# Differential attention: one group of eight value products an iteration in place of two groups of four

## What is computed

```
sc = einsum('bqhmd,bkhmd->bmhqk', q, k) * scale + bias     # two maps m = 0, 1
p  = softmax(sc, axis=-1)
a  = p[:, 0] - lam * p[:, 1]
o  = einsum('bhqk,bkhd->bqhd', a, v)                       # v: 64 columns a head
```

## Time and profile before

| | |
|---|---|
| median of 3 runs | 4055.61 us (4053.83 to 4058.95) |
| span of the profiled execution | 4058.1 us; what lies around it isn't listed |
| differential attention, layer 1 | 1182.8 us (first scores) to 1695.6 us (last output) |
| differential attention, layer 2 | 3206.8 to 3720.2 us, by the same pattern |
| granted clock of TensorE in the stage (1215 to 1680 us) | 1.00 (the 2.4 GHz level) |
| busy in that stretch of 465 us | PE 419.88, DVE 422.11, ACT 378.65, POOL 451.55 us |

### The profile page before, as it was taken

How to read it: one execution, slowest core, us unless ns; L and a number is a source line. 1 busy time by engine, 2 the same in 40 slices (tenths; PEclk the granted TensorE clock), 3 DMA queues, 4 the chain that set the end, 5 groups by cost and what they waited for, 6 DMA issues and landing times. The chain is left out here.

```text
span 4058.1 us, 51537 instructions
## 1 busy us (share of the span) xinstructions
PE 3793.6 (93%) x19002; PEld 2623.3 (65%) x19002; DVE 2243.3 (55%) x3973; ACT 1659.8 (41%) x2886; POOL 2463.3 (61%) x1381
## 2 busy tenths in 40 slices
PE   8999999999989899889989999999999889998898
PEld 7789774555545666557777897755555456665577
DVE  3002125555569999875530030255555699998755
ACT  3112103333348888761031021033333588887610
POOL 1221326877769999855512213267777699997555
PEclk9999999999999999999999999999999999999999
DMA  5433535233320222235353334422333202223353
GB/s 177 127 130 121 145 129 124 60 92 74 78 59 1 57 57 58 66 104 187 135 177 122 133 114 142 140 68 55 72 72 72 59 1 57 57 58 71 105 179 135
DMA packets 180864, 392.43 MB, mean 97 GB/s; under 512 B 18014, under 2 KB 100168, under 8 KB 168968
## 3 DMA queue, kind: packets, MB, share of 16 engines
q1 hardware_dynamic: 179752, 387.75, 34.1%
q10 hardware_dynamic: 864, 1.41, 0.2%
HBM read 255.93 MB, written 135.67 MB: 96 GB/s over the span
## 5 line engine op out<-in xcount | busy, mean ns | idle before, releaser
L1297 POOL TENSOR_TENSOR mla_sum_pool<-mla_sum_pool,mla_probs 128x1024 f32<-128x1024 f32 (+1 forms) x336 | 777.6, 2314 | 209.4 <-ACT mla_probs L1258 184.4
L1315 DVE TENSOR_REDUCE carry_row_max<-psum 128x1 f32<-128x512 f32 x688 | 474.5, 690 | 415.7 <-PE psum L1130 410.7
L1258 ACT ACTIVATE mla_probs<-psum 128x1024 f32<-128x1024 f32 x384 | 373.3, 1021 | 693.8 <-PE psum L1167 686.6
L1613 ACT ACTIVATE diff_probs<-psum,diff_shift 128x1024 f32<-128x1024 f32 x512 | 566.5, 1112 | 186.2 <-DVE diff_shift L1697 180.5
L1690 DVE TENSOR_REDUCE diff_row_max<-psum 128x1 f32<-128x1024 f32 x512 | 611.6, 1218 | 44.5 <-PE psum L1534 37.5
L1560 PE MATMUL psum<-ident,diff_probs 128*128 128x128 f32 x2048 | 328.3, 284 | 104.3 <-DVE diff_turned L1724 66.9
L638 PE MATMUL psum<-in_x_hi,in_w_hi 128*128 128x512 f32 x1024 | 409.9, 400 | 2.7 <-ACT in_mla_val L745 2.7
L638 PE MATMUL psum<-in_x_hi,in_w_lo 128*128 128x512 f32 x1024 | 405.8, 396 | 0.0
L638 PE MATMUL psum<-carry_firsts,in_w_hi 128*128 128x512 f32 x1024 | 404.6, 395 | 0.0
L1560 PEld LDWEIGHTS psum<-ident,diff_probs 128*128 128x128 f32 x2048 | 215.9, 141 | 280.1 <-issue 178.2
L1180 PE MATMUL psum<-mla_probs,mla_v_op 128*64 128x512 f32 x1536 | 374.8, 609 | 0.0
(11 more groups left out here) (213 smaller groups left out, 7408.7 us busy)
## 6 DMA issues: line engine op xcount, KB each, us to landing
in_w_raw<-in_w_in SPq DMA_DIRECT2D x64, 512.0 KB, 3.9
split_d<-in_out SPq DMA_DIRECT2D x64, 512.0 KB, 2.7
raw_d<-in_out SPq DMA_DIRECT2D x32, 512.0 KB, 2.6
mq_d<-in_out SPq DMA_DIRECT2D x48, 256.0 KB, 3.6
mk_d<-in_out SPq DMA_DIRECT2D x48, 256.0 KB, 3.9
carry_firsts<-split_d SPq DMA_DIRECT2D x48, 256.0 KB, 8.0
carry_weights<-split_d SPq DMA_DIRECT2D x48, 256.0 KB, 7.7
carry_weights<-split_d SPq DMA_DIRECT2D x16, 768.0 KB, 18.0
```

Of the source, the lines that this page charges most:

```text
L1258: nc.scalar.activation(probs[:, s % RING, :].rearrange("p (a n) -> p a n", n=CH), psum[:, S0 + 2 * (s % 2):S0 + 2 * (s % 2) + 2, :], ACT.E ...
L1297: nc.gpsimd.tensor_tensor(acc, start, probs[:, s % RING, mine], ALU.add).then_inc(pool_added, 1)
L1315: nc.vector.tensor_reduce(row_max[:, u % 2, qb, n:n + 1], psum[:, sweep_bank(g), :], AX.X, ALU.max).then_inc(maxed, 1)
L1613: nc.scalar.activation(dst[:, half * HALF:(half + 1) * HALF].rearrange("p (a n) -> p a n", n=CH), banks(n, m, half), ACT.Exp, bias=shift[: ...
```

## The change

`products` loses its argument `place` and goes through both chunks of eight key blocks at once. It is called once an iteration, between scores(n,1,0) and turns(n-2,1).

```
-                def products(n, place):
-
-                    g = (n - 4) // 2
+                def products(n):
+
+                    g, half = divmod(n - 4, 2)
                     if not 0 <= g < GROUPS:
                         return
-                    b, chunk = g // (NB // 2) % 2, 2 * ((n - 4) % 2) + place
-                    if chunk == 0 and g >= 1:
+                    b = g // (NB // 2) % 2
+                    if half == 0 and g >= 1:
                         pe.wait_ge(o_ready, g)
-                    pe.wait_ge(*copies(2 * g + 1, chunk))
-                    for kb in range(4 * chunk, 4 * chunk + 4):
-                        e = kb % 2
-                        last = nc.tensor.matmul(psum[e * DV:(e + 1) * DV, PV, 0:2 * P], v_op[b][:, kb, :],
-                                                turned[:, g % 2, kb, :], start=(kb < 2), stop=(kb >= NB - 2))
-                    if chunk == 3:
+                    for chunk in (2 * half, 2 * half + 1):
+                        pe.wait_ge(*copies(2 * g + 1, chunk))
+                        for kb in range(4 * chunk, 4 * chunk + 4):
+                            e = kb % 2
+                            last = nc.tensor.matmul(psum[e * DV:(e + 1) * DV, PV, 0:2 * P], v_op[b][:, kb, :],
+                                                    turned[:, g % 2, kb, :], start=(kb < 2), stop=(kb >= NB - 2))
+                    if half == 1:
                         last.then_inc(pv_done, 1)
...
                     if on:
                         scores(n, 0, 1)
-                    products(n, 0)
                     turns(n - LAG, 0)
                     if on:
                         scores(n, 1, 0)
+                    products(n)
                     turns(n - LAG, 1)
                     if on:
                         scores(n, 1, 1)
-                    products(n, 1)
                     turns(n - LAG, 2)
```

## The result

The changed kernel takes 4212.98 us (median of 4 runs, 4208.04 to 4217.4) against 4056.74 us before: ratio 1.0389, 95% interval 1.0376 to 1.0402. It is slower, 156 us, by more than the 124 us of the forecast and 3 us beyond its range. The profiled execution has a span of 4206.2 us, 148.1 more than that of before.

The account below looks back on a forecast made before the run. GpSimd was taken to bound the differential stage at 7.84 us a unit; a ring lengthened to 8.87 us gave 60 x (8.87 - 7.84) = 62 us a layer, 124 for two, so 4180 us, range 4125 to 4210.

Parts of the forecast that it names:

- What bounds the kernel before: Differential stage: GpSimd is the bound, with 7.69 us of instructions a unit and 7.78 us from unit to unit.
- The ring: Closed waits through VectorE, ScalarE and TensorE, maximum of scores(n,1,1) to the next: 8.84 us heavy, 8.90 light, against 7.84.
- The places of the waits: Differential stage: new waits of TensorE for ScalarE's copy, VectorE for scores(n,1,1), GpSimd for ScalarE's scale; 0.4 to 1 us each.
- E + 8.1: E is the start of the maximum of scores(n,1,1); VectorE's maximum of scores(n,1,0) was to end 8.1 us later.
- The drain keeps its order ..., worth under 1 us a layer: End of the differential stage: order kept but for unit 62's first transposes, under 1 us a layer either way.
- granted clock 1.0: Listed among the signs that the forecast is right: the granted clock stays at 1.0.
- The bounds of the ring's terms: Uncertainty of products, copy latency and shift: 124 - 35 to 124 + 18 us over 120 intervals, so 4145 to 4198.
- The rule weighed: TensorE tiling mode: fewer switches save 0.25 us an iteration; by the rule alone the time would be 4026 us.
- the 60 intervals of the sum: Intervals of the ring in iterations 4 to 63 that hold products: 60 x (8.87 - 7.84) = 62 us a layer.
- 1: Rival: TensorE's own work sets the pace, so saved switches come off, 30 us, to 4026; chance 2%.
- 2: Rival: GpSimd hides all of the insertion, so the time stays at 4056; chance 6%.
- 3: Rival: ScalarE's copy is no link, the ring through VectorE's copy(n-3,2) is longest, 40 us more, 4096; chance 10%.

Follow-up runs that it names:

- h: Kernel before, with ScalarE scaling 640 columns of a unit and GpSimd 384, in place of 512 and 512: 4049.99 us.
- j: Kernel before, with TensorE doing scores(n,0,1) ahead of turns(n-3,3), division of the scaling unchanged: 4084.76 us.
- f: Changed kernel, with the two matmuls of scores(n,0,0) issued twice, ahead of the wait for VectorE's copy(n-3,2): 4185.33 us.
- a: Kernel before, groups of four kept, only the first moved from before turns(n-2,0) to before turns(n-2,1): 4081.19 us.
- g: Changed kernel, with four of the eight products of an iteration left out: 4081.48 us.
- c: Changed kernel, with the eight products in one piece behind scores(n,0,1), before turns(n-2,0): 4148.69 us.
- e: Changed kernel, with ScalarE's copy(n-2,3) between the two exps of map 1 in place of behind both: 4182.43 us.

## Why the prediction was wrong, point by point

- **What bounds the kernel before.** GpSimd's work, as the forecast has it, is right by 0.04 us alone: in h this work fell by 0.21 us a unit and the pace from 7.84 to 7.80, where something else holds it. That this is a ring through the other engines is likely by j's 8.09, but it wasn't followed step by step.
- **The ring** of 8.84 and 8.90 us: right, 8.85 in the iteration shown and 8.86 as the mean of f. Its slack of 0.96 us against 1.96 inserted is borne out by a, g and f. 2 x 59 x (8.86 - 7.84) = 120 us.
- **The places of the waits**: right, their sizes too small. GpSimd's new wait was put at about 1 us a unit and is 72.3 us in 51 (1.4, with the slow stretches in it; in f 60.7 in 52, 1.2). The wait of turns(n-2,0) for ScalarE's copy was put at 0.4 to 0.5 us and is 0.35 to 0.94, 35.9 us in 51. The wait of the maximum of scores(n,1,1) was put at 0.9 us an iteration, 50 us a layer, and is 74.2 us in 51 (1.45; in f 65.4 in 52, 1.26); the other 19 of the 93 us are the maximum of scores(n,0,1), which waited 17 us before. The forecast let the maximum of scores(n,1,0) end near E + 8.1, by the rows of a heavy iteration; in the light one shown it ends at E + 7.5 (1516.59 + 1.21).
- **"The drain keeps its order ..., worth under 1 us a layer"**: wrong. From unit 62's ratio to the end of the last output pass 18.0 us before and 22.2 and 23.7 after (f: 23.3 and 22.1). In layer 1, of the 4.2 us more, 1.4 come up to the last band matmuls (1678.34 before, 1753.71 after), in the last turn of the ring, which ends behind that ratio. From there to the last 16 products pass 15.55 us in place of 12.72. Behind the last scores the pieces of products stand at other places too. Before, two transposes wait, 1.15 + 0.79 us:

```profile
1681.49 0.63 PE L1560 MATMUL psum<-ident,diff_probs 128*128 128x128 f32 x4 [1.15 <-DVE diff_turned L1724]
...
1683.92 1.09 PE L1560 MATMUL psum<-ident,diff_probs 128*128 128x128 f32 x8 [0.79 <-DVE diff_probs L1731]
```

In the changed kernel four do, 1.86 + 1.28 + 0.34 + 0.34 us:

```profile
1756.68 0.63 PE L1560 MATMUL psum<-ident,diff_probs 128*128 128x128 f32 x4 [1.86 <-DVE diff_turned L1724]
1758.58 0.65 PE L1560 MATMUL psum<-ident,diff_probs 128*128 128x128 f32 x4 [1.28 <-ACT diff_turned L1631]
1759.16 3.56 PE L1576 MATMUL psum<-diff_turned,diff_v_op 128*64 128x256 f32 x16
1762.65 1.09 PE L1560 MATMUL psum<-ident,diff_probs 128*128 128x128 f32 x8
1764.09 1.16 PE L1560 MATMUL psum<-ident,diff_probs 128*128 128x128 f32 x8 [0.34 <-ACT diff_turned L1631]
...
1768.49 0.63 PE L1560 MATMUL psum<-ident,diff_probs 128*128 128x128 f32 x4 [0.34 <-ACT diff_turned L1631]
```

The waits are 1.9 us more. The 16 records take 3.56 us here and 1.95 in the ring above: from 1758 to 1763 us the granted clock is 0.66, behind the waits of 1.86 and 1.28 us. That is another 1.6 us. Against it, one piece of four less stands in this stretch (1.0 us); the 0.3 us that are left weren't followed.

- **"granted clock 1.0"**: wrong, and this is the step that failed. The bounds of the ring's terms allowed for 18 us more; the clock was put at nothing, without a reason. The runs showed 0.97 in the stage and a cost of 27 us (4213 against f's 4185, which lies in the range). The drains added another 10 us where under 2 were allowed; without either of the two the time would have been within the range. That waits alone lower the clock isn't shown: in c and e TensorE waits too (it is busy in 380 and 379 of 465 us, in the changed kernel in 370), and their clock stays at 1.00 between the ratios.
- **The account.** In the profiled executions the interval between ratios 3 and 62 grew by 72.6 and 71.5 us in the two layers, the drains by 4.2 and 5.7; that is 154, and the span grew by 148. The stretch between the two differential stages is 5.7 us shorter (1515.9 against 1521.6 us), and it is so in a and f too, and more so in h (1514.9), which leaves the products where they were; so it doesn't come from their place alone. Why stays open.
- **The rule weighed.** The Trainium skill, TensorEngine Tiling (Array Packing), Key Properties, has it that a change of tiling mode drains TensorE. The trace agrees that one pair of switches fewer saves time: one piece of eight takes 1.88 us, two of four 2 x 1.01. It was no guide to the result: the gain is a small part of 1 us in a ring that got 1.96 longer.
- **Slips in the working.** Products run to iteration 67, not 65; the 60 intervals of the sum don't hang on it. Of these, 59 were measured at the ring's length, and the last, from ratio 62 to 63, grew by 0.3 us alone in layer 1 (6.60 to 6.90).
- **Rivals.** 1 and 2 are out. 3, in which ScalarE's copy is no link, is out by the waits on it in every iteration (0.94 us in the one shown), and by a, whose pace of 8.01 comes out of the ring through this copy.

## What to carry to other kernels

An instruction block's price depends on the ring of waits into which it is put: write down the rings that close once an iteration, with the slack of each against the pace, and insert only what the slack holds. When a block moves, look at what it covered at its old place, at every instruction queued behind it at the new one, and at the drain. If the change makes TensorE wait more, put a term for its clock into the upper end of the range: the forecast of this case had none, and the time went out of the range by 3 us.

## What I had not expected of the hardware

TensorE's clock fell in stretches inside a stage in which it was still busy 370 of 465 us (80%), each time costing about 1.4 us of an interval; with 0.55 us more work an iteration, work whose result is thrown away, the kernel got 28 us faster (4185.33 against 4212.98 us). It isn't simply the pace: e has 8.85 us an iteration, as f, with no added work and no slow stretch. What pattern of waits brings the fall stays open.
